# VectorE alone makes the lower parts of the second block's combined projection weights

## What is computed

```python
def mixer_ab(h, w_in, lb, hg_norm, w_out):
    proj = h @ w_in                       # 1024 x 3584
    qa, ka, va, qb, fb, ib, gb = jnp.split(proj, np.cumsum(AB_SPLITS)[:-1].tolist(), axis=-1)
    o_a = stick_breaking_attention(qa, ka, va)        # 8 heads of 64
    o_b = hgrn2(qb, fb, ib, lb)                       # 4 heads of 128, chunks of 64
    o_b = rmsnorm_2(o_b, hg_norm) * jax.nn.silu(gb)
    return jnp.concatenate([o_a, o_b], axis=-1) @ w_out

h = h + mixer_ab(rmsnorm_2(h, mix_norm[0]), ab_w_in[0], lower_bounds[0], hg_out_norm[0], ab_w_out[0])
```

## Time and profile before

| quantity | value |
|---|---|
| median of 3 runs | 1711.14 us |
| the profiled execution | 1705.77 us |
| its span in the trace | 1704.0 us |
| PE busy | 1433.7 us (84%) |
| DVE busy | 1014.5 us (60%) |
| ACT busy | 698.3 us (41%) |
| POOL busy | 896.7 us (53%) |

### The profile page before, as it was taken

How to read it: one execution, slowest core, us unless ns; L and a number is a source line. 1 busy time by engine, 2 the same in 40 slices (tenths; PEclk the granted TensorE clock), 3 DMA queues, 4 the chain that set the end, 5 groups by cost and what they waited for, 6 DMA issues and landing times.

```text
span 1704.0 us, 19456 instructions
## 1 busy us (share of the span) xinstructions
PE 1433.7 (84%) x6443; PEld 1027.4 (60%) x6443; DVE 1014.5 (60%) x1890; ACT 698.3 (41%) x1326; POOL 896.7 (53%) x826
## 2 busy tenths in 40 slices
PE   7877989888888876677779985889999968899998
PEld 5666884333333332222326865689987757799986
DVE  4675497666666666666543458546663485276743
ACT  5323522222233222223424632266546624566444
POOL 2212557777777777777753325065645450455614
PEclk9886999888888899999999998799999977899999
DMA  8812469999999999999996310466565440265560
GB/s 287 201 50 67 147 207 393 409 409 410 409 410 410 410 409 409 410 409 410 409 407 245 100 50 21 128 173 167 175 225 180 172 124 26 75 187 163 193 228 25
DMA packets 216878, 414.73 MB, mean 243 GB/s; under 512 B 13194, under 2 KB 117106, under 8 KB 216818
## 3 DMA queue, kind: packets, MB, share of 16 engines
q0 software_dynamic: 73728, 268.47, 39.8%
q1 hardware_dynamic: 142946, 145.46, 27.6%
q10 hardware_dynamic: 144, 0.04, 0.0%
HBM read 409.73 MB, written 4.19 MB: 243 GB/s over the span
## 4 chain that ended last, share of the span: by engine, by line
PE 43%; POOL 14%; DMA 13%; DVE 13%; issue 10%; ACT 4%; SPq 1%; POOLq 0%; DVEq 0%; ACTq 0%
PE ps L1792 12%; PE ps L1794 12%; PE ps L1793 12%; DMA expert_rows<-in_peer_u,route_idx 10%; POOL expert_rows L586 7%; POOL expert_rows L604 7%; DVE expert_rows L1441 3%; DMA weights_raw<-in_w_in 3%; PE ps L1935 1%; PE ps L1769 1%; ACT weights_hi L395 1%; DVE weights_lo L402 1%; PE ps L1921 1%; DMA expert_rows<-in_peer_v,route_idx 1%; PE ps L2015 1%
## 5 line engine op out<-in xcount | busy, mean ns | idle before, releaser
L2015 PE MATMUL ps<-expert_rows,proj 128*128 128x512 f32 x1024 | 505.6, 652 | 137.9 <-DMA expert_rows<-in_peer_v,route_idx 137.5
L2015 PEld LDWEIGHTS ps<-expert_rows,proj 128*128 128x128 f32 x1024 | 208.3, 209 | 434.5 <-issue 373.8
L1441 DVE CUSTOM_DVE_ANT_0 expert_rows<-expert_rows,ps 128x1024 f32<-128x1024 f32 x248 | 300.0, 1212 | 226.1 <-DMA expert_rows<-in_peer_u,route_idx 225.6
L542 POOL TENSOR_TENSOR weights_lo<-weights_raw,weights_hi 128x512 fp32r<-128x512 f32 x152 | 207.1, 1399 | 400.7 <-ACT weights_hi L395 376.6
L604 POOL DMA_INDIRECT expert_rows<-in_peer_u,route_idx x256 | 246.8, 964 | 104.0 <-issue 78.1
L586 POOL DMA_INDIRECT expert_rows<-in_peer_v,route_idx x256 | 245.0, 957 | 78.0 <-issue 74.0
L1792 PE MATMUL ps<-x_normT_hi,weights_hi 128*128 128x256 f32 x832 | 238.4, 287 | 9.0 <-DVE x_normT_lo L1129 9.0
L1793 PE MATMUL ps<-x_normT_lo,weights_hi 128*128 128x256 f32 x832 | 237.7, 286 | 0.0
L1794 PE MATMUL ps<-x_normT_hi,weights_lo 128*128 128x256 f32 x832 | 237.6, 286 | 0.0
L395 ACT CAST weights_hi<-weights_raw 128x2048 fp32r<-128x2048 f32 x94 | 177.0, 1916 | 130.0 <-PE ps L1794 81.1
L853 ACT ACTIVATE proj<-proj 128x4 f32<-128x4 f32 x64 | 13.1, 205 | 443.1 <-DVE proj L1441 443.1
(11 more groups left out here) (295 smaller groups left out, 2030.2 us busy)
## 6 DMA issues: line engine op xcount, KB each, us to landing
weights_raw<-in_ffn_up SPq DMA_DIRECT2D x88, 512.0 KB, 5.0
weights_raw<-in_ffn_down SPq DMA_DIRECT2D x22, 1024.0 KB, 5.0
weights_raw<-in_ab_w_in SPq DMA_DIRECT2D x14, 1024.0 KB, 5.2
weights_raw<-in_w_in SPq DMA_DIRECT2D x12, 1024.0 KB, 10.6
weights_raw<-in_peer_w_query SPq DMA_DIRECT2D x8, 1024.0 KB, 5.4
weights_raw<-in_ple_gate SPq DMA_DIRECT2D x8, 1024.0 KB, 6.3
weights_raw<-in_c_w_in SPq DMA_DIRECT2D x6, 1024.0 KB, 5.8
weights_raw<-in_w_out SPq DMA_DIRECT2D x4, 1024.0 KB, 6.2
```

The costliest lines, as they stand in the source:

```text
L542: ins = pool.tensor_tensor(w.lo[:, c], w.raw[:, c], w.hi[:, c].bitcast(F32), ALU.subtract)
L1441: ins = nc.vector.tensor_tensor_reduce(out=rows, in0=rows, in1=tokens, scale=1.0, scalar=0.0, op0=ALU.mult, op1=ALU.add, accum_out=r_dot[: ...
L2015: ins = pe.matmul(PS[:, (J[f"peer_{t}"] + m) % 8, :], DIAG[:, b % 2, k, :], vbuf[n][:, m * BANK:(m + 1) * BANK], start=False, stop=False, ...
```

## The change

The seven pieces leave GpSimd's program. VectorE makes the lower parts of pieces 2 and 3 right after the reciprocal of the second half's norm, and after chunk m of `ab` it makes both pieces of chunk m + 2 in place of the first alone.

```diff
@@ gpsimd
             pool.wait_ge(sem("rows_summed"), 4 * UNITS)
-            for p in (2, 3, 5, 7, 9, 11, 13):
-                split("ab", p)
             pool.wait_ge(sem("h_sufexp"), 1)
@@ evac_cols
                     if m + 2 < n and (name, m + 2) != ("win", 3):
-                        for p in {"c": halves(m + 2)[1:], "ab": halves(m + 2)[:1]}.get(name, halves(m + 2)):
+                        for p in {"c": halves(m + 2)[1:]}.get(name, halves(m + 2)):
                             split_lo(v, name, p)
@@ vector
             norm_rstd(1)
+            for p in halves(1):
+                split_lo(v, "ab", p)
             hq, hf, hi, hg = (proj_ab[:, :, 1536 + 512 * n:2048 + 512 * n] for n in range(4))
```

## The result

The changed kernel took 1716.94 us (median of 12 runs, 1714.0 to 1724.83), the kernel before 1705.72 us in the same comparison (median of 12, 1701.51 to 1715.2). The ratio is 1.0064 with a 95% interval from 1.0044 to 1.0085. So the change costs 11 us, and the interval allows 7.5 to 14.5 us. The sum of the prediction was +9.2 us.

A forecast was written before the change was run, and what follows sets the result against it. TensorE bounds the stage's first 71 us, so the split costs only where TensorE waits. 5.8 + 2.0 + 1.4 = +9.2 us gave 1715.0 from the profile, 1720.3 from the median; stated 1717.5, range 1709 to 1727.

The forecast's parts named there:

- What bounds the stage: First 71 us of the stage: TensorE bounds it, busy 68.54 of 71.2 us; the split costs only where TensorE waits.
- The head, +5.8: Stage's start: VectorE stands for ScalarE's upper part of piece 3, so TensorE's second tile starts 5.8 us later.
- Rival A: At the head: the wait for piece 3 is hidden, only 1.4 us stays, 1707 or 1712; chance 0.08.
- The clock, +2.0: Behind TensorE's longer head gap of 7.9 us: a lower granted clock costs 2.0 us, with a lower bound of 0.
- rival C: Behind the head gap: TensorE stays at half rate for two tiles, +19 us, 1725 or 1730; chance 0.08.
- The chain, +1.4: Around logits and softplus: pieces 9 and 13 add 2.2 us each, less 3.1 us relief; +1.4 us together, at most 4.4.
- The relief: At the absolute value and two softplus steps: with GpSimd silent, VectorE's instructions lose 1.07, 1.06 and 0.94 us, 3.1 together.
- Rival D: Around logits and softplus: the shortening from GpSimd's absence isn't there, +12.2 us in all; chance 0.08.
- Rival B: Before the second softplus: 3.1 us come off, added lower parts fall into idle time, 1702.7 or 1708; chance 0.04.
- GpSimd's removal, 0: Seven pieces, 28 instructions, about 39 us leave GpSimd; value zero, as TensorE's 0.56 us wait is covered by the 8.29 us one.
- All that follows moves as a block: After the product behind the softplus (988.38): work order is the old one on all engines and nothing is given back.
- The base: Starting time for the sum: profiled execution 1705.8 us or median of three timed runs 1711.1; the stated forecast lies between.

The follow-up runs named there:

- the head alone: Kernel before with only pieces 2 and 3 moved from GpSimd to VectorE at the head: 1714.48 us against 1708.7 (1.0038).
- the short fill: Changed kernel with eight products of zeros on TensorE before its second tile: 1819.99 us against 1811.82 for the kernel before (1.0041).
- the rest alone: Kernel before with pieces 5, 7, 9, 11 and 13 moved to VectorE, 2 and 3 left on GpSimd: 1713.13 us against 1708.7 (1.0017).
- the last version: Changed kernel with pieces 3, 9 and 13 behind normed rows, logits and softplus, plus GpSimd's wait in gated additions: 1707.78 us against 1706.0 (1.0008).
- the added wait: GpSimd waits for VectorE's last gate lower part in both gated additions; on the kernel before: 1711.47 us against 1706.0 (1.0025).
- the first experiment: Changed kernel with piece 3's lower part moved behind those of the normed rows: 1709.62 us against 1708.7 for the kernel before (1.0008).
- the kernel with three pieces behind: Changed kernel with pieces 3, 9, 13 behind normed rows, logits, softplus: 1707.33 us against 1708.7 (0.9982); repeated, 1809.69 against 1811.82 (0.9983).

## Why the prediction was right

**What bounds the stage.** Held. VectorE's total of busy time sets none of the loss; three places in its queue do. The prediction spoke of five covered pieces among the seven; its own list of three places leaves four (2, 5, 7 and 11), a slip in counting that no term rests on. They left no trace: piece 2's lower part is done at 912.53, before its successor's input exists, and over pieces 5 and 7 the delay goes from 7.69 (copy of the second tile) to 7.73 us (piece 8), and over piece 11 from 8.86 (piece 10) to 8.84 us (piece 12).

**The head, +5.8.** Measured 5.70, by a gap of 7.82 us where the prediction said 7.9. Undoing this piece alone took it away, and doing the head alone brought it back. Rival A falls.

**The clock, +2.0.** Measured 1.99 in the table and 1.95 by the short fill. Taking the price from the nearest gap in the trace, and not the length of time at half rate, was what kept rival C out: half rate lasted some 4 us here too. That the two agree to 0.1 us is partly luck, since in the second trace of the changed kernel the same gap cost 1.35 us. The lower bound of 0 rested on a clock of 1.00 behind the gap of 2.10 us. That wasn't a safe basis: in two later traces the clock was at half behind the same gap.

**The chain, +1.4.** Measured +1.36 with the rest alone, and 1.34 (9.03 - 7.69) in the changed kernel. The relief is 3.1 us in the three instructions, and 3.05 us in the end of the chain of the last version. Rival D falls with that. Rival B had the right relief, but it left out that piece 3 holds up the head, and that pieces 9 and 13 stand in front of the work that the relief speeds up. With all three behind, B's 3.1 us is what the stage gained in the one trace of three in which the clock stayed up; in the other two it was 1.5.

**GpSimd's removal, 0.** Right as a result. The 0.56 us are gone from before piece 11's tile, and are found again in the wait behind it. From 8.29 to 10.44 us this wait grew by 2.15, of which 0.56 is this and 1.34 the chain; 0.25 I can't place.

**"All that follows moves as a block."** Right up to the output projection (+9.16, after +9.03 at the product), and then not quite. The profiled execution had 4 us more in the first gated addition, from a meeting of VectorE and GpSimd whose length varies. Over 12 runs the median is 11.2 us later, 2.0 more than the sum, which lies within the interval of 7.5 to 14.5. With the meetings taken out of both kernels the medians differ by 8.7 us. That leans towards the meetings, but the intervals are too wide to say whether the rest is noise or more frequent long meetings.

**The base.** The three runs at first had a median of 1711.14 us, the twelve in the comparison 1705.72. The profiled execution's 1705.8 was the better base. From it the sum gives 1715.0, and from the median 1720.3; the stated 1717.5 lies between, 0.6 from the 1716.94 measured. That closeness is partly luck: the base was 2.6 us too high, and the sum 2.0 us too low. The prediction also took 1% for about what can't be told from none; with 12 runs of each the interval is 0.2% to either side, and the loss of 0.64% is clear of it.

**What to make of the change.** It makes one engine's work simpler to follow and costs 0.6%. The version with pieces 3, 9 and 13 behind the urgent work keeps VectorE alone on the lower parts and came to 0.9982 and 0.9983 in two comparisons, both with intervals that just include 1. It is level with the kernel before, or faster by some 1 to 3 us, and it is about 14 us faster than the changed kernel (0.9983 against 1.0059 in the comparison that has both).

## What to carry to other kernels

When work moves to an idle engine, don't ask how busy it is, but what stands behind the new instruction in its queue and when the new instruction's input is ready: 2.3 us of work cost 7.7 us here, of which 2.0 through the clock of the engine that had to wait, and a few places further down about 0.1. Two engines that slow each other are worth taking apart, but the gain only arrives if the moved work stands behind what it was slowing. And a wait added to get rid of a contention is itself such a move: it cost 2.8 us in each layer, most of it by the clock behind the new gap.

## What the runs showed of the hardware

**Turns for memory, several in a row.** VectorE's subtraction of 2048 columns takes 2.29 us alone. In meetings with GpSimd's subtractions of 512 columns it took 3.5, 4.75 or 5.95, which is 2.29 plus about one, two or three times 1.2 us. GpSimd's own take 1.26 us each undisturbed (5.02 for four; the earlier trace rows has them at 1.4 in the mean). GpSimd loses turns too: its four took 7.08 us beside the VectorE instruction of 3.48, and 5.02 beside the one of 5.97. The Trainium skill (SBUF — State Buffer, "SBUF: two separate sides") says that the loser of the shared port pair is blocked for the other's whole instruction; the traces agree, and add that VectorE can lose two or three turns in succession.

**A low clock behind a short gap.** Behind the same 2.10 us at the head the granted clock was 1.00 in the kernel before (with and without the added wait), in the first experiment, in the rest alone and in the kernel with three pieces behind and the added wait, and 0.50 to 0.53 in both traces of the kernel with three pieces behind. In the three kernels with the added wait TensorE stood 2.03 to 2.06 us in each gated addition, and a stretch of 3.4 us at half rate began behind five of these six gaps, 0.3 to 1.4 us after the restart. So a gap of 2 us is no assurance against the low clock. What decides I haven't found: the same placement with the later wait, which acts 400 us further on, had 1.00 at the head.

**Products of two float32 operands** ran as two instructions each: 16 instructions in 7.03 us, 0.44 us each, for 8 products of 512 columns.
